# Column sums of dA in the SSD branch: four fp32r products of ones with scaled triangles, in place of eight fp32 products

## The reference, cut to what matters

```
dt = softplus(dt_raw + dt_bias);  dA = dt * -exp(a_log)        # one value per row and head
a_cum = cumsum(dA, axis=rows of the chunk)
seg = a_cum[t] - a_cum[s];  decay = exp(where(s <= t, seg, -inf))
y_diag = einsum(C.B, decay, x)
```

## Time and profile before

| | us |
|---|---|
| median of three executions | 2528.74 |
| the profiled execution | 2530.42 |
| its span, from the first to the last instruction | 2528.8 |
| busy in it: PE, DVE, ACT, POOL | 2267.0, 1374.9, 980.1, 731.9 |
| column sums, line 443, all tiles, busy on PE | 34.7 |

### The profile page before, as it was taken

One profiled execution on the slowest core, in us unless ns is written; L12 is line 12 of the kernel. 1 busy time (PEld: TensorE's weight loads), 2 busy tenths in 40 slices (PEclk: granted clock), 3 DMA queues, 4 the chain that ended last, 5 costly groups with the idle time before them and its releaser, 6 DMA issues. The chain is left out here.

```text
span 2528.8 us, 35257 instructions
## 1 busy us (share of the span) xinstructions
PE 2267.0 (90%) x11464; PEld 1761.7 (70%) x11465; DVE 1374.9 (54%) x2803; ACT 980.1 (39%) x1730; POOL 731.9 (29%) x754
## 2 busy tenths in 40 slices
PE   4999999799999699999996989749999999999970
PEld 2899998577778455556554877638888888888850
DVE  2688888711100366666654677643355562435667
ACT  2566666311111145555555333222233451223433
POOL 0001110000000467777772011122233342223330
PEclk8999999799999699999997999869999999999995
DMA  6422121486762845544404644264567884557867
GB/s 221 183 79 87 71 83 53 174 275 229 263 217 99 180 109 106 102 103 95 91 10 140 203 150 134 80 224 100 174 199 240 281 291 116 155 141 235 277 210 281
DMA packets 191554, 408.40 MB, mean 162 GB/s; under 512 B 66490, under 2 KB 73960, under 8 KB 188032
## 3 DMA queue, kind: packets, MB, share of 16 engines
q1 hardware_dynamic: 153968, 272.98, 34.4%
q0 software_dynamic: 26704, 93.99, 13.7%
q10 hardware_dynamic: 10784, 40.18, 4.3%
HBM read 296.57 MB, written 110.53 MB: 161 GB/s over the span
## 5 line engine op out<-in xcount | busy, mean ns | idle before, releaser
L1416 POOL TENSOR_TENSOR c_acc<-c_acc,c_pr 128x512 f32<-128x512 f32 (+3 forms) x320 | 340.4, 1064 | 75.0 <-ACT c_pr L1538 34.2
L1538 ACT ACTIVATE c_pr<-c_ps,neg_f 128x512 f32<-128x512 f32 (+2 forms) x360 | 207.6, 594 | 162.6 <-PE c_ps L1482 156.8
L1568 DVE TENSOR_REDUCE c_mx<-c_pm 128x1 f32<-128x512 f32 (+3 forms) x304 | 178.8, 613 | 58.0 <-PE c_pm L1438 40.0
L1438 PE MATMUL c_pm<-c_km,c_q 66*128 66x512 f32 (+1 forms) x336 | 144.1, 445 | 22.8 <-DMA c_km<-f_k 16.2
L257 PE MATMUL p_zx<-wa_hi,ah_hi 128*128 128x432 f32 x408 | 154.4, 378 | 11.0 <-DVE wa_lo L252 7.2
L1491 PE MATMUL c_po<-c_pr,c_vv 128*64 128x512 f32 (+3 forms) x720 | 151.5, 523 | 0.0
L257 PE MATMUL x_pd<-x_d_hi,x_m_hi 128*128 128x512 f32 x344 | 140.6, 409 | 11.8 <-DVE x_m_lo L2530 11.8
L258 PE MATMUL p_zx<-wa_lo,ah_hi 128*128 128x432 f32 x408 | 148.5, 364 | 0.0
L259 PE MATMUL p_zx<-wa_hi,ah_lo 128*128 128x432 f32 x408 | 148.3, 363 | 0.0
L2443 ACT ACTIVATE x_sg<-x_pg 128x512 f32<-128x512 f32 x42 | 25.1, 597 | 316.4 <-PE x_pg L259 251.5
L634 POOL TENSOR_TENSOR yskip<-xs,params 128x512 f32<-128x512 f32 x17 | 26.4, 1551 | 415.2 <-ACT xs L559 415.2
(11 more groups left out here) (396 smaller groups left out, 5702.5 us busy)
## 6 DMA issues: line engine op xcount, KB each, us to landing
x_raw_g<-in_w_gate_dram SPq DMA_DIRECT2D x32, 1024.0 KB, 7.3
x_raw_u<-in_w_up_dram SPq DMA_DIRECT2D x32, 1024.0 KB, 7.6
x_raw_d<-in_w_down_dram ACTq DMA_DIRECT2D x30, 1024.0 KB, 8.4
b_wa<-in_w_ada_dram POOLq DMA_DIRECT2D x16, 1024.0 KB, 7.1
c_k<-k_hi SPq DMA_DIRECT2D x14, 672.0 KB, 14.0
h_hi<-ah_hi SPq DMA_DIRECT2D x17, 512.0 KB, 2.6
h_lo<-ah_lo SPq DMA_DIRECT2D x17, 512.0 KB, 3.4
d_mix<-mix SPq DMA_DIRECT2D x17, 512.0 KB
```

Source lines behind the costliest of these rows:

```text
L1416: pool.tensor_tensor(acc[:, ci % 2, cols], acc[:, ci % 2, cols], pr[:, i % RING, cols], ALU.add).then_inc(acc_done, 1)
L1438: last = pe.matmul(p_m[x % 2][:, 0:w * P], q2[0:KR, s, u["tile"] * P:(u["tile"] + 1) * P], km[:, s, kc], start=True, stop=not masked)
L1538: act.activation(pr[:, n % RING, cols], p_s[n % NPS][:, cols], ACT.Exp, bias=c.neg_f[:, it["h"], it["key"]:it["key"] + 1]).then_inc(exp_do ...
L1568: dve.tensor_reduce(mx[:, u % 2, pc["slot"]:pc["slot"] + 1], src, AX.X, ALU.max).then_inc(mx_done, 1)
```

## The change

The column sums are computed another way round. The stationary operand is now a matrix of ones, `ones_r`, and the moving operand is the triangle with each row r scaled by dA[r, head], for four heads at once (512 columns). In fp32r these products keep fewer bits of an operand, so dA is split into a rounded high part and the rest, `dA_hl`, and there is a scaled triangle for each: `steps_hi` and `steps_lo`, 8 heads each. They have the places in memory of seg and mm. ACT makes them with sixteen copies of `tri` that take a column of dA_hl as the scale, behind its conv products. DVE makes dA_hl behind dA with two small instructions, and ones_r once at the start. PE has the additional wait steps_ready, ACT waits for dlo_ready (the split), m_ready (seg has been read) and yd_done (mm has been read).

```
 pe.wait_ge(conv_first, i)
-for hh in range(H):
-    last = pe.matmul(p_h[:, hh * P:(hh + 1) * P], dA[:, hh:hh + 1].to_broadcast([P, P]), c.tri[:], start=True, stop=True)
+pe.wait_ge(steps_ready, i)
+for half in range(2):
+    out, hs = p_h[:, half * 512:half * 512 + 512], slice(4 * half, 4 * half + 4)
+    pe.matmul(out, ones_r[:], steps_hi[:, hs, :], start=True, stop=False)
+    last = pe.matmul(out, ones_r[:], steps_lo[:, hs, :], start=False, stop=True)
 last.then_inc(at_done, 1)
...
 last.then_inc(conv_first, 1)                                    # ACT, end of step
+act.wait_ge(dlo_ready, i + 1)
+for part, steps in enumerate((steps_hi, steps_lo)):
+    if back:
+        act.wait_ge((m_ready, yd_done)[part], i)
+    for hh in range(H):
+        last = act.activation(steps[:, hh, :], c.tri[:], ACT.Copy, scale=dA_hl[:, part, hh:hh + 1].bitcast(F32))
+last.then_inc(steps_ready, 1)
...
 dve.tensor_tensor(dA[rows, :], t(0)[rows, 0:H], c.neg_a[rows, :], ALU.mult).then_inc(dt_ready, 1)
+dve.wait_ge(dt_ready, i + 1)
+if back:
+    dve.wait_ge(steps_ready, i)
+dve.tensor_copy(dA_hl[:, 0, :], dA[:]).then_inc(dhi_ready, 1)
+dve.wait_ge(dhi_ready, i + 1)
+dve.tensor_tensor(dA_hl[:, 1, :], dA[:], dA_hl[:, 0, :].bitcast(F32), ALU.subtract).then_inc(dlo_ready, 1)
```

More of the change, by code:

```diff
@@ L282, in ssd_branch @@
         w_hi, w_lo = weights
+        with (nc.sbuf_tensor("steps_hi", [P, H, P], F32R, align_bytes=LINE) as steps_hi,
+              nc.sbuf_tensor("steps_lo", [P, H, P], F32R, align_bytes=LINE) as steps_lo):
+            pass
         seg, mm = sb("seg", [P, H, P]), sb("mm", [P, H, P])
@@ L298, in ssd_branch @@
         b_tok = sb("b_tok", [P, P])
+        ones_r, dA_hl = sb("ones_r", [P, P], F32R), sb("dA_hl", [P, 2, H], F32R)
         state, cdl = sb("state", [P, DS]), sb("cdl", [P, 4])
@@ L322, in ssd_branch @@
         qh_loaded = sem("qh_loaded")
+        onesr_ready, dhi_ready, dlo_ready, steps_ready = map(sem, ("onesr_ready", "dhi_ready", "dlo_ready", "steps_ready"))
         block = ctx.enter_context(nc.Block())
@@ L441, in step @@
                     pe.wait_ge(conv_first, i)
-                    for hh in range(H):
-                        last = pe.matmul(p_h[:, hh * P:(hh + 1) * P], dA[:, hh:hh + 1].to_broadcast([P, P]), c.tri[:],
-                                         start=True, stop=True)
+                    pe.wait_ge(steps_ready, i)
[3 more added lines that the diff above has]
+                        last = pe.matmul(out, ones_r[:], steps_lo[:, hs, :], start=False, stop=True)
                     last.then_inc(at_done, 1)
@@ L499, in _ @@
             step(0, back=False)
+            pe.wait_ge(onesr_ready, 1)
             with pe.Fori(1, LAST - 1) as i:
@@ L784, in step @@
                     last.then_inc(st_ready, 1)
+            dve.tensor_copy(ones_r[:], c.ones[:]).then_inc(onesr_ready, 1)
             dve.memset(xraw[:, :, 0:CW - 1], 0.0).then_inc(conv_step, 1)
```

## The result

The changed kernel takes 2593.9 us (median of four runs, 2565.3 to 2599.2), the kernel before on the same chip 2530.9. The ratio, formed from all the runs and not from the two medians, is 1.0229, 95% interval 1.0181 to 1.0276: slower, as forecast, but by 63 us between the medians where 23 to 25 were expected; the time lies 21 us above the upper end of the range. The four runs are in the order of their mean granted clock: 2565.3 at 0.937, 2593.3 and 2594.5 at 0.924, 2599.2 at 0.922.

A forecast was written before the change was run, and what follows sets the result against it. PE's own work, busy for all 22.60 us, was taken to set a step of the SSD branch. Fifteen steps 1.59 us longer plus one 1.12 longer made 25.0 us, hence 2553.7 us, range 2540 to 2573.

The forecast's parts named there:

- rival C: PE's clock in the branch falls because PE stands idle 2.4 us in every step; 2629 us, chance 0.03.
- The rival's price: On PE, the 24 products of group 1 at the lower clock: 4.7 us more a step, 75 us in all.
- The wait itself: PE waits before the sums for ACT's last copy: a stall of 2.38 us, the step 1.59 us longer, 24.2 us.
- The 0.07 us taken for the pointer: On ACT, what a scale read from a tile adds to a copy's spacing, giving 0.275 us per copy.
- the full 1.59 us: Lengthening charged to each of fifteen steps: PE's stall less its saving on the sums.
- The four products: On PE, four fp32r products of 512 columns replace eight fp32 ones: 0.91 us instead of 1.70.
- DVE: DVE idles 2.5 us before the mean; its 0.54 us idle and slack before PE's transposes cover the split.
- the 0.2 us reckoned: Margin by which xbc, ready at 279.9, precedes PE's need at 280.1: no second stall.
- A: ACT's copies are cheap: about 2529 us, or 2516 with all saved; chance 0.05 without a gain, 0.03 with (shared with D).
- B: ACT's copies cost 0.342 us like conv products, 2571 us, or DVE's late xbc overtakes PE; chance 0.11.
- D: ACT reaches the copies earlier, so they don't bind and the saving is real; chance 0.03, shared with A's gain.
- The last tile: Step 17 has no projections to cover the copies; zero to 4.4 us possible, taken as zero.

The follow-up runs named there:

- e1: Changed kernel with ten fp32r products of 512 columns put on PE ahead of its wait for the copies, in steps 1 to 16; 2558.8 us, ratio 1.0099.
- e5: Changed kernel with a constant as the copies' scale instead of a column of dA, so the sums are not dA's; 2556.2 us, ratio 1.0093.
- e9: Changed kernel with the low part summed by eight fp32r products ahead of the wait, and only the high part copied; 2527.1 us, ratio 0.9985.
- e6: Changed kernel with two of the sixteen copies made by POOL and fourteen by ACT; 2552.9 us, ratio 1.0089.
- e4: Changed kernel with the scaled triangles made by POOL in two multiplications instead of ACT's sixteen copies; 2556.1 us, ratio 1.0105.
- e7: Changed kernel with POOL making both the scaled triangles and the split of dA; 2553.8 us, ratio 1.0098.
- e3: Changed kernel with the eight old fp32 products back in place of the four new ones, copies and wait kept; 2593.2 us, ratio 1.0235.
- e2: Changed kernel with the low part of dA left out of the sums, leaving eight copies and two products; 2524.4 us, ratio 0.9969.

## Why the prediction was wrong

**The failed step: rival C.** The prediction named the fall of the clock, gave it a chance of 0.03 and set it aside because "Idle time of 2.2 us did not do it"; its sum has no term for the clock. In the profiled execution the clock took 39.5 of the 66.3 us. Those 2.2 us, in the stretch from 80 to 88 us of before, were not one pause: 1.64 us lie before the transposes at 84.62, 0.58 before group 0 at 86.06, with work between. The new wait is one pause of 2.55 us, and it was followed by a lower clock in all of one trace's 14 steps with it and in 8 of 14 in another's. The stretch from 452 us, at 0.70, had spoken for the rival, and was left without a consequence.

The trace of before also had a single pause of this kind inside the branch, which speaks against the rival. PE there, and then the stretch behind the pause (columns as above):

```profile
417.24 0.65 PE L452 MATMUL p_xs<-ident,xbc 128*128 128x128 f32 x4 [3.02 <-ACT xbc L553]
```

```profile
417.00:420.00 3.00, 2.76 (x17) 2.42 (x18) 3.00 (x10) 2.94 (x8) 0.50 (x1) 1.00 0.00 0
```

After 3.02 us the clock was still at 1.00. So the rows of before could not have settled whether the new wait lowers the clock. They showed that a pause sometimes does and sometimes does not, and the step that failed is to have put the clock's term at nothing on one stretch that held two short pauses.

**The rival's price was also wrong, in the other direction.** It let all 24 products of group 1 run at half speed, 4.7 us a step; the measured price is 27.3 - 24.5 = 2.8 us where the clock is down at the restart, and 26.1 - 24.5 = 1.6 where it falls after it. In the first case the lower level lasts about six microseconds from the restart: it adds 1.84 - 1.02 = 0.82 us to the sums (1.02 is what they take in e1) and 12 x 0.16 = 1.9 to the first twelve products of group 1. The trace of before had a row for that. PE there, where the next stage begins after a pause (PEq is PE's own sequencer):

```profile
482.41 0.77 PE L257 MATMUL b_pu<-b_h_hi,wb_hi 128*128 128x512 f32 x1 [4.71 <-PEq L60]
482.97 0.63 PE L258 MATMUL b_pu<-b_h_lo,wb_hi 128*128 128x512 f32 x1
483.40 0.63 PE L259 MATMUL b_pu<-b_h_hi,wb_lo_early 128*128 128x512 f32 x1
...
487.92 0.40 PE L258 MATMUL b_pu<-b_h_lo,wb_hi 128*128 128x512 f32 x1
488.15 0.39 PE L259 MATMUL b_pu<-b_h_hi,wb_lo_early 128*128 128x512 f32 x1
```

The first twelve products start 0.43 apart, the later ones 0.23: 12 x 0.2 = 2.4 us after a pause, not 4.7. With it the rival would have stood at 2553.7 + 16 x 2.4 = 2592.1 us, 1.8 below what was measured, and the range would have had to reach there. That it comes so near is partly luck: the wait was 0.34 us a step longer than forecast, and the same kernel took 2578.9 us the second time.

**The wait itself: right in place, a size off.** PE waits for ACT's last copy sixteen times, behind it no other wait, as forecast. A copy starts 0.292 us after the one before, not 0.275, the last takes 0.415 (the mean of the group), not 0.38, and PE woke 0.15 us after it ended, not 0.10: 15 x 0.017 + 0.035 + 0.05 = 0.34 us a step. That makes 24.5 of the forecast 24.2, which is the step of e1 and, within 0.1, that of the seven steps of the second trace whose clock stayed up. The 0.07 us taken for the pointer from copies out of PSUM was too low, as e5 showed 0.09. The estimate of 0.293 us per copy, which the prediction worked out beside its sum from the figures of the Trainium skill's page "ScalarE: Activation LUTs", section "What ACT_TABLE_LOAD costs", agrees with the measured 0.292. The sum also charged the full 1.59 us to the step whose sums start at 407.56 in before, where PE waited 3.02 us for xbc anyway; e1 is only 0.1 us longer there than before.

**The four products: right at the upper level.** 0.91 us forecast; 1.02 in e1, where the spacing behind the first one is included.

**DVE: right.** 2.74 us of idle time before the mean (2.5 forecast), released by junk; the split covered by the idle time before the modulation; xbc in time for PE, which with its step 4.7 us longer had more room than the 0.2 us reckoned.

**Rivals A, B and D** did not happen: the copies are neither cheap nor at 0.342, and PE's wait is no shorter than ACT's copies make it. B's second half, a late xbc on PE, brought nothing new: the kernel before waits for xbc twice in its last steps (3.02 and 1.39 us), e1 twice (1.18 and 0.92), the changed kernel once (0.3 us in step 17).

**The last tile: right.** Of the seventeen sums only sixteen wait; the copies of step 17 cost nothing.

## What to carry to other kernels

A new wait on TensorE has two prices: its length, and the clock after it, to be read from the spacing of products behind single pauses, and behind many of them, not from the busy share of a stretch that adds several up: one pause of 3.02 us left the clock up, most of those of 2.6 us did not. Where a wait can't be avoided, put work that doesn't need its result ahead of it (e9), or take some tenths of a microsecond out of it (e6; at 2.0 to 2.2 us the clock still fell now and then, e4 and e7), and look at the next products' spacing for what that gave. Idle time on another engine counts only between the release and the need, and work given to POOL was paid for by DVE here, in the pair of instructions with two SBUF inputs that ran beside it (e4, e7).

## What the runs showed of the hardware

- Of the pauses ahead of the sums, the longer ones were followed by a lowered clock more often: in 0 of 14 steps at 1.86 to 1.90 us (e6), 2 of 11 at 2.00 to 2.02 (e4), 4 of 10 at 2.15 to 2.17 (e7), 12 of 14 at 2.59 (e3), and at 2.55 to 2.59 in 14 of 14 steps of one trace of the changed kernel and 8 of 14 of another. None of these lengths is a bound by itself: the one pause of 3.02 us before xbc in the kernel before left the clock up (at the same place it fell in all seven runs of e2 and e4 to e9 that pause there, for 2.0 to 4.1 us), and the 1.89 us of step 1 in the changed kernel, where PE had paused before the transposes and group 0 as well, for 1.64 and 1.00 us, seven to nine microseconds earlier, were followed by a fall.
- The clock can fall after the restart: in five steps of the two traces of the changed kernel 0.9 to 1.5 us of products ran at the upper level first, in e3 up to 1.4 us.
- It came back some six microseconds after the restart where it was down at the restart, and 4.3 to 4.9 us after it in those five steps, with the same products. A fall of the first kind cost 2.8 us, one of the second 1.6, and one in e3 1.6. Why they differ was not tried.
- POOL's multiplication of 128x1024 beside DVE's subtractions: 3.61 and 3.80 us for a pair that takes 1.30 alone.
